# Hybrid attention and pooling step: new order of the front, six row tiles ahead of the first adaptive part

## What is computed

```python
mod = jax.nn.silu(c) @ w_ada + b_ada
shift, scale, gate = jnp.split(mod, 3, axis=-1)
h = _layer_norm(x) * (1.0 + scale[:, None, :]) + shift[:, None, :]
proj = h @ w_in                  # q 512 | k 128 | v 128 | g_attn 512 | u 512 | g_pool 512
...                              # rotary, banded attention with sinks, multi-scale trailing means
mixed = jnp.concatenate([o_attn * silu(g_attn), o_pool * silu(g_pool)], axis=-1)
r = DN_ALPHA * x + gate[:, None, :] * (mixed @ w_out)
y = _layer_norm(r) * ln_g + ln_b
```

## Time and profile before

| | us |
|---|---|
| median of three runs | 450.83 (450.24 to 451.83) |
| the profiled execution | 454.2 |
| its span, first to last instruction | 452.4 |
| TensorE busy, share | 431.4, 95% |
| VectorE, ScalarE, GpSimd busy | 272.1, 124.6, 139.3 |
| mean granted TensorE clock | 0.978 |

### The profile page before, as it was taken

The page is one execution under the profiler, slowest core; times in us unless marked ns, Lnnn a source line. Parts: engine busy times, 40 slices in busy tenths (PEclk is TensorE's granted clock), DMA queues, the critical chain, the costliest instruction groups (busy, mean ns, idle before and its releaser), DMA issues.

```text
span 452.4 us, 6736 instructions
## 1 busy us (share of the span) xinstructions
PE 431.4 (95%) x2604; PEld 371.4 (82%) x2604; DVE 272.1 (60%) x531; ACT 124.6 (28%) x305; POOL 139.3 (31%) x108
## 2 busy tenths in 40 slices
PE   4899989999999999999999999999989999999993
PEld 1466979889999998978988888898967778888883
DVE  6355685420127666436765653776495887888875
ACT  4353551212210001533333353433461100000000
POOL 2446652102223220264233122421292333333300
PEclk9589999999999999999999999999998999999998
DMA  8998600608211301101200120110482022222231
GB/s 300 422 419 344 233 1 1 232 2 263 104 49 49 113 28 48 53 8 48 53 2 7 47 53 6 48 20 35 110 266 96 1 93 94 93 93 94 93 131 55
DMA packets 23687, 47.59 MB, mean 105 GB/s; under 512 B 12068, under 2 KB 14500, under 8 KB 22344
## 3 DMA queue, kind: packets, MB, share of 16 engines
q1 hardware_dynamic: 23656, 47.16, 30.0%
HBM read 41.71 MB, written 6.36 MB: 106 GB/s over the span
## 4 chain that ended last, share of the span: by engine, by line
PE 85%; DVE 7%; ACT 3%; DMA 2%; issue 2%; SPq 1%; DVEq 0%
PE proj_ps L659 13%; PE proj_ps L661 13%; PE proj_ps L660 13%; PE proj_ps L795 8%; PE proj_ps L797 8%; PE proj_ps L796 8%; PE s_ps L556 2%; PE s_ps L695 2%; PE t_ps L724 2%; DMA wada<-w_ada 2%; PE t_ps L585 2%; PE proj_ps L612 2%; PE proj_ps L625 2%; PE proj_ps L613 2%; DVE Pb L1211 2%
## 5 line engine op out<-in xcount | busy, mean ns | idle before, releaser
L659 PE MATMUL proj_ps<-h_hi,w_hi 128*128 128x384 f32 x384 | 132.8, 346 | 0.0
L660 PE MATMUL proj_ps<-h_lo,w_hi 128*128 128x384 f32 x384 | 129.1, 336 | 0.0
L661 PE MATMUL proj_ps<-h_hi,w_lo 128*128 128x384 f32 x384 | 129.1, 336 | 0.0
L1331 POOL TENSOR_TENSOR w_lo<-w_raw,w_hi 128x1024 fp32r<-128x1024 f32 x16 | 41.3, 2580 | 157.2 <-ACT w_hi L908 157.2
L659 PEld LDWEIGHTS proj_ps<-h_hi,w_hi 128*128 128x128 f32 x384 | 72.2, 188 | 4.1 <-issue 2.2
L660 PEld LDWEIGHTS proj_ps<-h_lo,w_hi 128*128 128x128 f32 x384 | 72.2, 188 | 0.8
L661 PEld LDWEIGHTS proj_ps<-h_hi,w_lo 128*128 128x128 f32 x384 | 72.2, 188 | 0.0
L795 PE MATMUL proj_ps<-wo_hi,m_hi 128*128 128x512 f32 (+1 forms) x152 | 59.4, 391 | 0.2 <-issue 0.2
L797 PE MATMUL proj_ps<-wo_hi,m_lo 128*128 128x512 f32 (+1 forms) x152 | 59.0, 388 | 0.0
L796 PE MATMUL proj_ps<-wo_lo,m_hi 128*128 128x512 f32 (+1 forms) x152 | 59.0, 388 | 0.0
L1130 DVE SCALAR_TENSOR_TENSOR mixed<-th,proj_ps 128x384 f32<-128x384 f32 x24 | 13.3, 553 | 48.5 <-ACT th L922 48.5
(11 more groups left out here) (156 smaller groups left out, 637.0 us busy)
## 6 DMA issues: line engine op xcount, KB each, us to landing
w_raw<-w_in SPq DMA_DIRECT2D x18, 512.0 KB, 4.2
wada<-w_ada SPq DMA_DIRECT2D x8, 1024.0 KB, 17.4
xs<-x_all SPq DMA_DIRECT2D x9, 512.0 KB, 12.1
xf<-x_all SPq DMA_DIRECT2D x9, 512.0 KB, 4.0
wada_late<-w_ada SPq DMA_DIRECT2D x2, 2048.0 KB, 8.3
y_out<-yr SPq DMA_DIRECT2D x8, 512.0 KB, 2.9
wo_raw<-w_out SPq DMA_DIRECT2D x4, 512.0 KB, 3.3
wo_rest<-w_out SPq DMA_DIRECT2D x4, 512.0 KB, 8.5
```

Source lines behind the costliest of these rows:

```text
L659: pe.matmul(bank[:, 0:CW], w_hi[:, w, k, :], hi, start=(k == 0), stop=False)
L660: pe.matmul(bank[:, 0:CW], w_hi[:, w, k, :], lo, start=False, stop=False)
L661: mm = pe.matmul(bank[:, 0:CW], w_lo[:, w, k, :], hi, start=False, stop=(k == KT - 1))
L1331: pool.tensor_tensor(w_lo[:, b % 2], w_raw[:, b % RAW], w_hi[:, b % 2].bitcast(F32), ALU.subtract).then_inc(wlo_done, 1)
```

## The change

- **SP:** the small loads go ahead of x2, x3 to x5 ahead of adaptive part 0, x6 and x7 ahead of part 3.
- **VectorE and GpSimd** do statistics and `inv_std` of six tiles in one go; ScalarE normalises tiles 0 to 4, VectorE tile 5, all ahead of part 0.
- **Transposes** 2 and 3 go into banks of their own. Slices tau 4 to 15 (`EARLY`) are copied from PSUM into SBUF tiles `xT`, even ones by ScalarE, odd ones by VectorE (`early_copy`), and `h_full` reads them there. A transpose then waits for the copy of its bank, not for `hx`. The tiles lie where `Pb`, `PT1`, `PT2`, `kT`, `th` and `Vs` live later; a `memset` of `PT2` moves behind unit 4 for that.
- **TensorE:** seven `keep_busy` in place of four at the start, then transposes 0 and 1, and further ones between the halves of part 0. `first_products` does the first products of units 0 to 3 by weight part. `x_transpose(6, 7)` and `low_pair(1, 0)` now stand ahead of `ada(1)`; `low_pair(0, 3)` and `high_pair(1, 3)` ahead of `x_transpose(16, 17)`.

```diff
--- before.py
+++ after.py
@@ -147,6 +147,7 @@
 SPARE_UNIT = 2
 BANK_BEFORE = {5: 3, 6: 0}
 DVE_LOW = (1, 2)
+EARLY = range(4, 16)
 
 
 def hi_count(x):
@@ -247,9 +248,19 @@
     kT = place("kT", [P, TOK])
     th = place("th", [P, 2, CW])
     r_ks = top[0]
+    xT = {}
+    for m, k in enumerate(range(2, 5)):
+        xT[("p", 0, k)] = place(f"xT0_{k}", [P, CW], at=r_p + 4 * CW * m)
+        xT[("p", 0, k + 3)] = place(f"xT0_{k + 3}", [P, CW], at=r_k + 4 * CW * m)
+        xT[("p", 1, k)] = place(f"xT1_{k}", [P, CW], at=r_p + 4 * CW * (3 + m))
+    for m, k in enumerate(range(5, 7)):
+        xT[("p", 1, k)] = place(f"xT1_{k}", [P, CW], at=r_k + 4 * (TOK + CW * m))
+    assert 6 * CW * 4 <= r_k - r_p and TOK == 3 * CW
     Ks = place("Ks", [P, NSP, 2, WIN])
     hs = place("hs", [P, 2, KT // 2, P], at=r_ks)
+    r_vs = top[0]
     Vs = place("Vs", [P, NSP, 2, P])
+    xT[("p", 1, 7)] = place("xT1_7", [P, CW], at=r_vs)
     r_u = region(3 * UB * 4)
     rt1 = place("rt1", [P, 2, CW], at=r_u)
     rt2 = place("rt2", [P, 2, CW], at=r_u + 2 * CW * 4)
@@ -342,6 +353,8 @@
     ada_done = sem("ada_done"); sel_done = sem("sel_done"); xt_done = sem("xt_done"); unit_done = sem("unit_done")
     vt_done = sem("vt_done"); s_done = sem("s_done"); t_done = sem("t_done"); pv_done = sem("pv_done"); y_done = sem("y_done")
 
+    xc_a = sem("xc_a"); xc_v = sem("xc_v"); xn_v = sem("xn_v")
+
     thc_done = sem("thc_done"); xn_done = sem("xn_done"); ada_evac = sem("ada_evac"); hs_done = sem("hs_done")
     hhi_done = sem("hhi_done"); whi_done = sem("whi_done"); act_free = sem("act_free"); th_done = sem("th_done")
     exp_done = sem("exp_done"); es_done = sem("es_done"); pt1_done = sem("pt1_done"); mhi_done = sem("mhi_done")
@@ -362,6 +375,11 @@
 
     def unit_bank(n):
         return s_ps[:, 0, :] if n == SPARE_UNIT else proj_ps[:, 2 if n == SPARE_UNIT + 1 else n % 3, :]
+
+    def transposed_bank(tau):
+        if tau == 2:
+            return s_ps[:, 0, :]
+        return proj_ps[:, 2, :] if tau == 3 else t_ps[:, tau % 2, :]
 
     def w_low_done(eng, b):
         if b in DVE_LOW:
@@ -425,21 +443,21 @@
 
             load_x(0)
             load_x(1)
-            load_x(2)
             sp.dma_start(ident[:], ident_d).then_inc(ld_id, 16)
             sp.dma_start(sel[:], sel_d).then_inc(ld_id, 16)
             sp.dma_start(bT[:], bT_d).then_inc(ld_id, 16)
+            load_x(2)
+            load_x(3)
+            load_x(4)
+            load_x(5)
             load_ada(0)
             load_w(0)
             load_w(1)
-            load_x(3)
-            load_x(4)
-            load_x(5)
             load_ada(1)
             load_ada(2)
-            load_ada(3)
             load_x(6)
             load_x(7)
+            load_ada(3)
             load_x(8)
             load_w(2)
             sp.dma_start(cosT[:], cos_d).then_inc(ld_cs, 16)
@@ -568,21 +586,28 @@
             def x_transpose(*taus):
                 for tau in taus:
                     kind, c, k = T_ORDER[tau]
-                    b = tau % 2
+                    b = transposed_bank(tau)
                     if tau == 0:
                         pe.wait_ge(ld_id, 48)
-                    if tau >= 2:
+                    elif tau in (4, 5):
+                        pe.wait_ge(hx_done, tau - 3)
+                    elif 6 <= tau < 18:
+                        pe.wait_ge(xc_v if tau % 2 else xc_a, (tau - 4) // 2)
+                    elif tau >= 18:
                         pe.wait_ge(hx_done, tau - 1)
                     if kind == "s":
-                        pe.wait_ge(xn_done, TILES)
+                        pe.wait_ge(xn_done, TILES - 1)
                         for i in range(4):
                             m = 4 * k + i
-                            mm = pe.transpose(t_ps[:, b, P * i:P * (i + 1)], xs[:, TILES - 1, P * m:P * (m + 1)], ident[:])
+                            mm = pe.transpose(b[:, P * i:P * (i + 1)], xs[:, TILES - 1, P * m:P * (m + 1)], ident[:])
                     else:
                         for t in range(3 * c, min(3 * c + 3, TILES - 1)):
-                            pe.wait_ge(xn_done, t + 1)
+                            if t == 5:
+                                pe.wait_ge(xn_v, 1)
+                            else:
+                                pe.wait_ge(xn_done, t + 1 - (t > 5))
                             i = t - 3 * c
-                            mm = pe.transpose(t_ps[:, b, P * i:P * (i + 1)], xs[:, t, P * k:P * (k + 1)], ident[:])
+                            mm = pe.transpose(b[:, P * i:P * (i + 1)], xs[:, t, P * k:P * (k + 1)], ident[:])
                     mm.then_inc(xt_done, 1)
 
             def wait_bank(n):
@@ -613,6 +638,19 @@
                     pe.matmul(bank[:, 0:CW], w_lo[:, w, k, :], h_hi[:, c, k, :], start=False, stop=False)
                     if taus:
                         x_transpose(taus.pop(0))
+
+            def first_products(n, part):
+
+                c, b = n // 2, block_of(n)
+                if part is w_hi:
+                    pe.wait_ge(whi_done, b + 1)
+                else:
+                    w_low_done(pe, b)
+                if n == 3:
+                    pe.wait_ge(hx_done, 4)
+                for k in range(2):
+                    pe.wait_ge(hhi_done, hi_count(("p", c, k)))
+                    pe.matmul(unit_bank(n)[:, 0:CW], part[:, b % 2, k, :], h_hi[:, c, k, :], start=(part is w_hi and k == 0), stop=False)
 
             def low_products(n, slices):
                 kind, j, c = UNITS[n]
@@ -798,43 +836,53 @@
                     if k == KT - 1:
                         mm.then_inc(y_done, 1)
 
-            keep_busy(4)
-            ada(0)
+            keep_busy(7)
             x_transpose(0, 1)
+            keep_busy(2)
+            ada(0, range(0, 4))
+            keep_busy(2)
+            ada(0, range(4, KT))
+            keep_busy(1)
             select(0)
             keep_busy(1)
-            high_pair(0, 0)
-            low_pair(0, 0)
-            keep_busy(2)
+            x_transpose(2, 3)
+            first_products(0, w_hi)
+            first_products(1, w_hi)
+            first_products(0, w_lo)
+            x_transpose(4, 5)
+            first_products(2, w_hi)
+            low_products(0, (0, 1))
+            first_products(3, w_hi)
+            first_products(1, w_lo)
+            low_products(1, (0, 1))
+            first_products(2, w_lo)
+            first_products(3, w_lo)
+            x_transpose(6, 7)
+            low_pair(1, 0)
             ada(1)
-            x_transpose(2, 3)
+            x_transpose(8, 9)
             select(1)
-            x_transpose(4, 5)
-            high_pair(1, 0)
-            low_pair(1, 0)
+            x_transpose(10, 11)
             ada(2)
-            x_transpose(6, 7)
+            high_pair(0, 1)
+            x_transpose(12, 13)
             select(2)
-            high_pair(0, 1)
-            x_transpose(8, 9)
+            low_pair(0, 1)
             high_pair(1, 1)
-            low_pair(0, 1)
-            x_transpose(10, 11)
+            x_transpose(14, 15)
+            low_pair(1, 1)
             ada(3)
-            low_pair(1, 1)
             high_pair(0, 2)
             select(3)
-            x_transpose(12, 13)
+            low_pair(0, 2)
             high_pair(1, 2)
-            low_pair(0, 2)
-            x_transpose(14, 15)
+            low_pair(1, 2)
             high_pair(0, 3)
-            low_pair(1, 2)
+            low_pair(0, 3)
+            high_pair(1, 3)
             x_transpose(16, 17)
-            high_pair(1, 3)
-            low_pair(0, 3)
+            low_pair(1, 3)
             x_transpose(18, 19)
-            low_pair(1, 3)
             x_transpose(20, 21)
             high_products(4, range(KT), range(22, len(T_ORDER)))
             low_products(4, range(KT))
@@ -900,6 +948,11 @@
                         act.wait_ge(hx_done, tau + 1)
                         i = LOW_ORDER.index(HI_ORDER[m])
                         act.activation(h_hi[:, c, k, 0:pw], hx[:, i % HX, 0:pw], ACT.Copy).then_inc(hhi_done, 1)
+
+            def early_copy(*taus):
+                for tau in taus:
+                    act.wait_ge(xt_done, tau + 1)
+                    act.activation(xT[T_ORDER[tau]][:], transposed_bank(tau)[:, 0:CW], ACT.Copy).then_inc(xc_a, 1)
 
             def w_high(b):
                 act.wait_ge(ld_w[b % RAW], 16 * (b // RAW + 1))
@@ -971,21 +1024,23 @@
 
             act.wait_ge(ld_c, 16)
             act.activation(thc[:], cT[:], ACT.Tanh, scale=0.5).then_inc(thc_done, 1)
-            normalise(0)
-            normalise(1)
-            normalise(2)
+            for t in range(5):
+                normalise(t)
             evac_ada(0)
             w_high(0)
             w_high(1)
-            h_high(0, 1)
-            normalise(3)
-            normalise(4)
-            normalise(5)
+            h_high(0, 1, 2, 3)
+            early_copy(4, 6)
             evac_ada(1)
-            h_high(2, 3, 4, 5)
```

(57 more changed lines are left out.)

## The result

The changed kernel takes 453.91 us (median of 8 runs, 452.56 to 455.06), the kernel before 450.65 in runs beside it (8 runs, 448.61 to 451.93). The ratio is 1.0056, 95% interval 1.0031 to 1.0081: it is slower, by about 2.5 us by the ratio and 3.3 us by the medians. The prediction said 450.1 us, with 452.5 as the upper end.

What follows compares the result with a forecast made beforehand. TensorE, 95% busy, was taken as the bound, with a 28 us front under a transfer and half clock and a group-3 tail paced by VectorE. Gains of 0.4 + 0.34, about 0.75 us, off 450.83 gave 450.1 us, range 447.9 to 452.5.

Steps and rivals of the forecast that it cites:

- The sum's base: Whole kernel: the difference formed in the profiled span of 452.4 us was applied to the median of 450.83.
- the walk: Step-by-step timing of the new order through the front to the third group's tail; about 0.75 us less.
- TensorE is 3.3 us ahead: At `ada(1)`: 3.9 us of work less to do, started 0.6 us late, so a lead of 3.3 us.
- Transfers: Front loads: 1.5 MB of x3 to x5 ahead of part 0 take 3.8 us; part 3 landing later costs nothing.
- The wait at `low_products(0)`: Near 25 us: VectorE and GpSimd hold each other up, and TensorE stands about 1.1 us.
- The third group: Waits for `h_hi` and `h_lo` add 0.7 to 1.9 us; sample transposes start at 53.7, 0.4 us earlier.
- The tail: From the first sample transposes to the last `hx` pair: about 0.34 us shorter, VectorE waiting less for a transpose.
- `hx` from SBUF: VectorE's `hx` read from SBUF: 0.3 us in place of 0.6, or most of the gain lost to waits for GpSimd.
- the lower bound: Third group: `hx` from SBUF takes 0.3 us and meets no GpSimd work, so sample transposes start at 53.1.
- The clock falls all the same: Rival, chance 0.15: half clock in the front from 13.1 to 26.75 us; end 3.2 to 4.3 us later, 454.5.
- the main case: Front and tail together: 0.4 + 0.34, about 0.75 us less, 450.1 us; chance 0.55 for 449.2 to 450.8.
- The side engines keep up: Rival, chance 0.22: no hold-up by VectorE, GpSimd, ScalarE; sample transposes near 51.2, 3.3 us less, 447.5.

Runs made afterwards that it cites:

- before_again: The kernel before run once more with no edit, for a second profile: 450.24 us, ratio 1.0002.
- light_fill: The kernel before with few zero products added (five at the start, one between the halves of part 0, one between first products): 449.94 us, ratio 0.9962.
- x2_first: The changed kernel with tile 2 of x loaded ahead of the three small loads again: 453.96 us, ratio 1.0077 to the kernel before.
- tail_first: The changed kernel with transposes 16, 17 ahead of low_pair(0, 3) and 18, 19 ahead of low_pair(1, 3): 451.26 us, ratio 1.0023 to the kernel before.
- filled_x_ahead: before_filled with x3 to x5 loaded ahead of adaptive part 0 and ten zero products at the start: 455.34 us, ratio 1.0082 to the kernel before.
- both: The changed kernel with the edits of x2_first and tail_first together: 452.12 us, ratio 1.0023 to the kernel before.
- after_unfilled: The changed kernel without its added zero products in the front: 454.98 us, ratio 1.0096 to the kernel before.
- loads_back: The changed kernel with load and side-engine order of before ahead of modulation 0, light_fill's zero products and tail_first's tail order: 455.03 us, ratio 1.0116.
- before_filled: The kernel before with zero products added in its front gaps (six at the start, others around part 0 and the first products): 451.59 us, ratio 0.9999.

## Why the prediction was wrong

**The sum's base was the failing step.** "I form a difference in the span and apply it to the median" is right where the profiled execution loses what the median one loses. It didn't. I saw that the profiled execution was 3.4 us over the median and treated it as an offset. It was the half clock: 13.65 us of it in front and a stretch of 3.4 us at 341 us, a mean of 0.978, against 0.989 for the typical execution (6.9 us, all in front, in before_again). The gain of the change, full clock in front, was thus counted against a loss that the median has only in part. Not all of the 3.4 us lies in front: from unit 6 to the end the profile of before takes 381.8 us, before_again, without the stretch at 341 us, 380.0. The table of clocks puts it in numbers: from 452.4 to typically 449 the kernel before had already 3.4 us less. Against its own base the walk was off by far less: unit 6 was to start 0.75 us ahead of the profile of before, at 69.9; typically it starts at 70.95, 0.3 behind it. Of the 3.8 us between 450.1 and 453.9, 3.4 are the base (454.2 less 450.83). The walk is 1.1 us off at unit 6, and what follows unit 6 took some 0.5 less than in the profile of before (381.3 for 381.8), so about 0.5 is left of it: the same walk on the base of its own execution gives 454.2 - 0.75 = 453.45, for 453.91 measured.

**"TensorE is 3.3 us ahead" falls with it.** It compared `ada(1)` at 28.85 with 28.27 of an execution at half clock. Measured against the order of before at full clock, with both profiles free of half stretches before the last us (light_fill, whose spans at 0.996 are those of the kernel before, against x2_first), the account is:

| | light_fill | x2_first | later by |
|---|---|---|---|
| `select(0)` | 15.26 | 19.97 | 4.7 |
| `ada(1)`, with 3.9 us of work ahead of it that the order of before has behind | 24.11 | 29.58 | 5.5 |
| sample transposes | 50.12 | 54.86 | 4.7 |
| unit 6 | 66.55 | 70.95 | 4.4 |

The 3.9 us of work done ahead make up for most of `ada(1)`'s delay, and leave TensorE 1.6 us behind there, not 3.3 ahead. At unit 6 it is 4.4 us: 2.0 of the tail order (tail_first), and 2.4 that remain of the load order's 3.6 to 3.8.

**Transfers: the size right, the cover wrong.** 3.8 us was the estimate for 1.5 MB ahead of part 0; filled_x_ahead measured 3.6 on TensorE, and tail_first against light_fill 3.8 at the first half of part 0. But I let the half clock hide it: under half clock TensorE would have been late anyway. With the clock held, part 0 is what TensorE waits for, in both orders (the releaser of the first `ada` row is a `wada` transfer at 11.01 in light_fill, at 14.81 in tail_first), and in filled_x_ahead the delay goes through whole. That small loads ahead of x2 cost nothing is confirmed by x2_first and both. Part 3 behind x6 and x7 wasn't waited for either.

**The wait at `low_products(0)`** was to be 1.1 us from the mutual exclusion of VectorE's `w_lo` and GpSimd's `h_lo`. It is there, at its place (27.19, and 26.11 in x2_first), at 0.63 to 0.67 us. VectorE's `w_lo` takes 1.27 us there, hardly more than the 1.22 alone; it is GpSimd that is held up, with four `h_lo` in 4.91 us against 3.92 alone:

```profile
24.17 4.91 POOL L1408 TENSOR_TENSOR h_lo<-hx,h_hi 128x384 fp32r<-128x384 f32 x4
```

**The third group: mechanism and size right.** Waits for `h_hi` behind `normalise(7)` and for `h_lo` behind `inv_std(8)` were named, 0.7 to 1.9 us. The profile after has them, 0.58 and 0.52, together 1.1, and so has x2_first. TensorE, GpSimd and ScalarE in order of time:

```profile
51.18 0.44 PE L637 MATMUL proj_ps<-h_hi,w_hi 128*128 128x384 f32 x1 [0.58 <-ACT h_hi L950]
```

```profile
50.89 0.73 POOL L1391 TENSOR_TENSOR rstd<-veps,mhalf 128x1 f32<-128x1 f32 x1 [1.46 <-DVE veps L1100]
...
51.85 3.92 POOL L1408 TENSOR_TENSOR h_lo<-hx,h_hi 128x384 fp32r<-128x384 f32 x4
```

```profile
49.47 1.24 ACT L929 ACTIVATE xs<-xs,nmr,rstd 128x1024 f32<-128x1024 f32 x1 [1.52 <-POOL nmr L1394]
50.62 0.92 ACT L950 ACTIVATE h_hi<-hx 128x384 fp32r<-128x384 f32 x2
```

The transposes were forecast for 53.7, at most 54.3; typically they start at 54.86, since TensorE came 0.6 us later to `select(0)` (19.97 for 19.4), 0.7 later to `ada(1)` and 0.8 later to `ada(3)` (42.36 for 41.55). That 2.2 us of work stand ahead of them was in the text as the place where the lead goes. What I didn't do is price the reverse: with `x_transpose(16, 17)` and `(18, 19)` one step earlier, the kernel is 2.0 us shorter. I had the lead as spent, when it was the order that spent it.

**The tail** was to be 0.34 us shorter from the first transposes to the last `hx` pair. It is 8.60 (55.89 to 64.49) for 8.92: 0.32. Right, though 8.6 lies under the 8.8 that the text itself named as a sign of being wrong; its own sum, 8.92 less 0.34, was there already.

**`hx` from SBUF.** The question left open was 0.3 us or the wait for GpSimd. VectorE in order of time, pairs of `hx` from `xT`:

```profile
34.68 0.87 DVE L1148 TENSOR_SCALAR hx<-xT,s1T,shT 128x384 f32<-128x384 f32 x2
...
35.94 2.24 DVE L1148 TENSOR_SCALAR hx<-xT,s1T,shT 128x384 f32<-128x384 f32 x2
...
40.34 1.88 DVE L1148 TENSOR_SCALAR hx<-xT,s1T,shT 128x384 f32<-128x384 f32 x2
```

```profile
35.87 2.09 POOL L1408 TENSOR_TENSOR h_lo<-hx,h_hi 128x384 fp32r<-128x384 f32 x2 [6.79 <-ACT h_hi L950]
```

With GpSimd idle a pair takes 0.87 us, 0.43 for each, against 1.26 from PSUM: a gain, but short of the 0.3 of the lower bound. The pair at 35.94, beside GpSimd's `h_lo` from 35.87 to 37.96, takes 2.24. The rows agree with both of the pages that the prediction cites: the Trainium skill's "VectorE: DVE Perf Modes" (What auto-detection actually checks) on the faster mode from SBUF, and its "SBUF — State Buffer" (SBUF: two separate sides) on the exclusion. Of the six pairs four take 0.86 to 1.13 us, so gain 0.1 to 0.4, and the two beside GpSimd lose 0.6 and 1.0.

**The rivals.** "The clock falls all the same" did not come true: both profiles, after and x2_first, have full clock in front, and no execution of the changed kernel has a mean under 0.992. Its argument from busy shares isn't borne out either: from 9.70 to 13.10 TensorE is busy 1.33 of 3.40 us in the profile after, 39% where 57% was forecast, and the clock stayed full, though before it had fallen behind one stretch of 53%. The price was too high for the clock itself: 6.5 us less 2 to 3, where after_unfilled with the half clock on some 13 us is 1.5 longer than the changed kernel at 0.996. (With the 0.75 us of the main case taken off, these terms give 2.8 to 3.8 over the kernel before, and not the 3.2 to 4.3 of the text.) That after_unfilled took 454.98, near the rival's 454.5, is luck: the price was too high and the base too low. "The side engines keep up" did not come true either; its 51.2 for the transposes is near tail_first's 51.96, which took another order and no faster engine. What I lacked was a rival on the base: that the profiled execution is not the typical one. Its place was in sight, in the 3.4 us between 454.2 and 450.83.

**What stays open.** Of the 4.1 us at equal clock the tail order's 2.0 are shown, and the load order's 3.6 in the kernel before. That the transposes and products made ahead give back the 1.2 to 1.5 us between is a difference of these, not an experiment: loads_back, made to show it, brought a wait of its own. Why the half clock lies on 13.65 us in one execution of the kernel before and on 6.9 in another isn't settled, nor is why 39% busy kept the clock here and 53% didn't there.

## What to carry to other kernels

Ask of a profile first whether it is a typical execution: where its time lies over the median by as much as the effect to be forecast, find what that excess consists of (here the mean granted clock, 0.978 against 0.989) and take it out of the sum before a gain is counted against it. With TensorE waiting for a load, as here for part 0, bytes put ahead of that load delay it by their transfer time (3.6 us in filled_x_ahead), and only work that the order then really does earlier can give some of it back; count that against the time at full clock, where no half clock covers the delay. Work that is ahead should be used to start the next stage that another engine paces: here the transposes first and the products behind them, for 2.0 us.

## What the runs showed that was not expected

- The kernel before, unchanged, has spans from 446.5 to 452.4 us, and these go with the mean granted clock, 0.996 to 0.978: (452.4 - 446.7) over 17 us of half clock (13.65 and 3.4), about a third of a us for each us of it.
- In the front of the changed kernel, where TensorE waits for loads, the half clock costs little: some 13 us of it made the kernel 1.5 us longer (after_unfilled). One stretch of 3.4 us at 341 us, where TensorE has no such wait, costs about as much: the changed kernel's spans are 452.0 to 453.3 with a mean clock of 0.992 or 0.993, the profile after among them, and 450.85 without.
- Three more zero products, spread over the front, cost nothing in the spans at an equal clock and made the half clock rarer (light_fill, 0.38% faster than before by the ratio); eight more cost 1.6 us (before_filled).
